# Two slots for the low halves of weights instead of three, five raw slots instead of four, and a new order of heads, ups and rope tables

## The reference

```python
def first_block(x, ...):                       # one layer
    u = rmsnorm(x, norm_mix)
    u_ssm, q, k, v = split(u @ w_in)           # 4 x 512
    y_ssm = s5_branch(u_ssm, ...)              # complex state space, 32 groups x 64 states, gelu,
                                               # y * sigmoid(y @ w_glu + b_glu)
    y_attn = stick_breaking_attention(q, k, v) # 8 heads of 64: z = q.k, w = exp(log_sigmoid(z)
                                               #   + sum of log_sigmoid(-z) over later keys)
    g_ssm, g_attn = split(sigmoid(u @ w_gate + b_gate))
    merged = g_ssm * (y_ssm @ w_up_ssm) + g_attn * (y_attn @ w_up_attn)
    h = x + merged @ w_out
    hid = relu(rmsnorm(h, norm_mlp) @ w_ff1)   # 1024 -> 4096
    h = h + (hid * hid) @ w_ff2
    return rmsnorm(h, norm_final)

def second_block(x, c, positions, ...):        # two layers
    cos, sin = rope_tables(positions)
    for l in range(2):
        shift, scale, gate = split(silu(c) @ w_ada + b_ada)
        u = x * (1 + scale) + shift
        a_in, a_gate, b_in, b_gate, q_lat, kv_lat, k_rope, c_gate, merge = split(u @ w_in)
        y_a = (silu(layer_norm(conv31(a1 * sigmoid(a2)))) * silu(a_gate)) @ w_a_out
        y_b = (gb * conv3(gc * xb) * silu(b_gate)) @ w_b_out
        y_c = (latent attention with rope, 8 heads * silu(c_gate)) @ w_c_out
        m = sum of sigmoid(merge parts) * (y_a, y_b, y_c)
        x = layer_norm(alpha * x + gate * (m @ w_o))
    return x
```

## Time and profile before

| | |
|---|---|
| median of 3 runs | 1069.53 us (1066.78 to 1070.15) |
| the profiled execution | 1071.31 us, of which the span is 1069.6 us |
| mean granted TensorE clock | 0.98 of full |
| instructions | 19601 |

### The profile page before, as it was taken

One profiled execution on the slowest core, in us unless ns is written; L12 is line 12 of the kernel. 1 busy time (PEld: TensorE's weight loads), 2 busy tenths in 40 slices (PEclk: granted clock), 3 DMA queues, 4 the chain that ended last, 5 costly groups with the idle time before them and its releaser, 6 DMA issues.

```text
span 1069.6 us, 19601 instructions
## 1 busy us (share of the span) xinstructions
PE 1020.7 (95%) x8132; PEld 960.3 (90%) x8132; DVE 696.7 (65%) x1052; ACT 545.7 (51%) x631; POOL 376.4 (35%) x159
## 2 busy tenths in 40 slices
PE   7998999889999999999999999999999999999996
PEld 6985777779899999989999999999789999999995
DVE  4958788773435322345977986856449789877563
ACT  5455554744544444446654744644366456446442
POOL 3079673003487888710056530000100456300000
PEclk8998999999999999999999999999899999999998
DMA  8642444664774656553744555554556444564601
GB/s 278 197 159 81 157 157 159 222 212 158 242 231 126 194 193 187 186 175 123 237 129 148 161 175 178 160 195 158 153 163 203 153 130 150 182 192 147 209 19 40
DMA packets 159496, 179.58 MB, mean 168 GB/s; under 512 B 5040, under 2 KB 141744, under 8 KB 159408
## 3 DMA queue, kind: packets, MB, share of 16 engines
q1 hardware_dynamic: 159024, 177.22, 52.0%
q0 software_dynamic: 384, 1.10, 0.3%
HBM read 177.26 MB, written 1.05 MB: 167 GB/s over the span
## 4 chain that ended last, share of the span: by engine, by line
PE 76%; DVE 9%; issue 7%; ACT 5%; DMA 2%; POOL 1%; SPq 0%; DVEq 0%; ACTq 0%; POOLq 0%
PE pg L1791 64%; DVE p_bu L1669 2%; ACT w_hi L924 2%; PE p_s L1874 2%; DVE area L1243 2%; PE p_y L1949 1%; ACT u_hi L899 1%; PE pg L1812 1%; PE p_s L1767 1%; DVE area L1261 1%; PE p_s L1928 1%; DVE rows L1285 1%; DVE area L1247 1%; DMA area<-in_c_state 1%; PE p_bu L1928 1%
## 5 line engine op out<-in xcount | busy, mean ns | idle before, releaser
L814 POOL TENSOR_TENSOR w_lo<-raw,w_hi 128x2048 fp32r<-128x2048 f32 x61 | 285.3, 4688 | 316.9 <-ACT w_hi L924 316.9
L924 ACT ACTIVATE w_hi<-raw 128x2048 fp32r<-128x2048 f32 (+3 forms) x153 | 275.1, 1804 | 67.5 <-PE pg L1791 29.3
L1234 DVE TENSOR_TENSOR w_lo<-raw,w_hi 128x2048 fp32r<-128x2048 f32 (+2 forms) x92 | 190.7, 2084 | 61.0 <-ACT w_hi L924 60.8
L1791 PE MATMUL pg<-u_hi,w_hi 128*128 128x256 f32 x1536 | 213.5, 291 | 16.7 <-ACT u_hi L899 11.0
L1791 PEld LDWEIGHTS pg<-u_hi,w_hi 128*128 128x128 f32 x1536 | 195.9, 193 | 27.2 <-issue 11.4
L1791 PE MATMUL pg<-u_lo,w_hi 128*128 128x256 f32 x1536 | 202.9, 285 | 0.0
L1791 PE MATMUL pg<-u_hi,w_lo 128*128 128x256 f32 x1536 | 200.2, 283 | 0.0
L1791 PEld LDWEIGHTS pg<-u_lo,w_hi 128*128 128x128 f32 x1536 | 194.3, 195 | 0.0
L1791 PEld LDWEIGHTS pg<-u_hi,w_lo 128*128 128x128 f32 x1536 | 191.4, 192 | 0.0
L930 ACT ACTIVATE area<-pg 128x512 f32<-128x512 f32 (+1 forms) x92 | 54.1, 588 | 155.5 <-PE pg L1791 143.6
L1669 DVE SCALAR_TENSOR_TENSOR p_bu<-area,par,p_bu 128x256 f32<-128x256 f32 x232 | 93.9, 483 | 0.8
(11 more groups left out here) (221 smaller groups left out, 1343.6 us busy)
## 6 DMA issues: line engine op xcount, KB each, us to landing
raw<-in_w_in SPq DMA_DIRECT2D x68, 1024.0 KB, 5.4
raw<-in_w_ff SPq DMA_DIRECT2D x32, 1024.0 KB, 5.6
raw<-in_w_ada SPq DMA_DIRECT2D x24, 1024.0 KB, 5.3
raw<-in_w_gate SPq DMA_DIRECT2D x8, 1024.0 KB, 7.8
raw<-in_w_o SPq DMA_DIRECT2D x8, 1024.0 KB, 5.2
raw<-in_w_out SPq DMA_DIRECT2D x4, 1024.0 KB, 8.7
raw<-in_w_b_out SPq DMA_DIRECT2D x4, 1024.0 KB, 5.1
raw<-in_w_c_out SPq DMA_DIRECT2D x4, 1024.0 KB, 5.5
```

The source lines that it names most:

```text
L814: pool.tensor_tensor(w_lo[:, s, 0:n], raw[:, r, 0:n], w_hi[:, s, 0:n].bitcast(F32), ALU.subtract).then_inc(sem(f"raw_free{r}"), 1)
L924: act.activation(dst, src, ACT.Copy).then_inc(*(c.event("w_hi", q["s"]) if i == len(parts) - 1 else c.step()))
L1234: ins = dve.tensor_tensor(dst, src, hi.bitcast(F32), ALU.subtract)
L1791: ins = pe.matmul(pg[g % 2][0:m, i * T:i * T + T], w[:, k, a:a + m], x[:, k, :], start=x is x_hi and w is wh and (i, k) == turns[0], stop= ...
```

## The change

`raw` gets five slots, `w_lo` two (`LO`), `w_hi` keeps three. The window of the look-ahead is a constant of its own (`AHEAD` = 4), so the halves are issued as far ahead as before. The low halves of `up_attn` 0 and 1, `up_ssm` 0 and 1, `out` 0 and 1 and `glu` 0 move from VectorE to GpSimd (68 there instead of 61). The bu matmuls no longer stand between the two z matmuls of `stick_scores`; the outputs of two heads are made together (`stick_out` for even heads only, once for two). `high_ahead` stands before `s5_y`. `rope_tables` is cut in four steps, one after each of the ff1 panels 4 to 7, and `modulate_columns` comes two chunks later. The weights, products and bytes are the same.

```diff
@@ slots and the list
-POOL_LOW = [("gate", n) for n in range(3, 8)] + [(job, n) for job in ("ff1", "ff2") for n in range(2 * DFF // W)]
+POOL_LOW = [("gate", n) for n in range(3, 8)] + [(job, n) for job in ("up_attn", "up_ssm", "out") for n in range(2)] + [("glu", 0)] + [(job, n) for job in ("ff1", "ff2") for n in range(2 * DFF // W)]
-RAW = 4
+RAW = 5
 HL = 3
+LO = 2
+AHEAD = 4
@@ the order: heads
         if m + 1 < HEADS:
             step("stick_scores", m + 1)
-        else:
-            step("bu", 2 * m + 1)
+        step("bu", 2 * m + 1)
...
+        if m and m % 2 == 0:
+            step("stick_out", m - 2)
...
-        if m:
-            step("stick_out", m - 1)
-    step("stick_out", HEADS - 1)
+    step("stick_out", HEADS - 2)
     step("ada_turn", 10)
     step("s5_out", HEADS - 1)
     step("split", "ctx")
+    step("high_ahead", count["split"] + 2)
     step("s5_y", WT - 1)
...
-    step("high_ahead", count["split"] + 2)
@@ the order: feed-forward
                 panel("ff1", 0, 2 * c + n, "w_ff1", 0, W * c + 256 * n, KT, 256, 1)
+                if c in (2, 3):
+                    step(("rope_angles", "rope_reduced", "rope_half", "rope_tables")[2 * c - 4 + n])
...
-        if c == 2:
-            step("rope_tables")
+        if c == 4:
             step("modulate_columns", 0)
@@ the waits of a low half (GpSimd, and VectorE alike)
-                    past = SPLIT[q["s"] - HL]
+                    past = SPLIT[q["s"] - LO]
                     pool.wait_ge(sem("groups"), past["g"] + past["groups"] - 1 + 1)
...
-            within = RAW if PANELS[at]["split"] else 1 if PANELS[at]["layer"] and PANELS[at]["n"] in (7, 11) else 2
+            within = AHEAD if PANELS[at]["split"] else 1 if PANELS[at]["layer"] and PANELS[at]["n"] in (7, 11) else 2
@@ TensorE, heads
             def stick_scores(hd, _):
...
-                if hd:
-
-                    bu_ready(2 * hd - 1)
-                    bu_part(2 * hd - 1, 0)
                 pe.matmul(p_z[:, 0:T], k1[rows, f, 0:P], q1[rows, f, :], start=True, stop=True)
-                if hd:
-                    bu_part(2 * hd - 1, 1).then_inc(*event("bu", 2 * hd - 1))
                 pe.matmul(p_z[:, T:T + P], k1[rows, f, P:T], q1[rows, f, P:T], start=True, stop=True).then_inc(*event("z", hd))
...
             def stick_out(hd, _):
-                pe.wait_ge(sem("w_stick"), over("w_stick", hd))
+                pe.wait_ge(sem("w_stick"), over("w_stick", hd + 1))
...
-                weighted_values(v1, stick_w[:, hd % 2], hd).then_inc(*event("o_stick", hd))
+                weighted_pair(v1, stick_w, hd).then_inc(*event("o_stick", hd // 2))
@@ VectorE, rope
-            def rope_tables(_, __):
+            def rope_angles(_, __):
...
                 ts(nmean[rows], nmean[rows], freq[rows, 0:1], None, ALU.mult).then_inc(*c.step())
+            def rope_reduced(_, __):
                 turns(nmean[rows], sin_cos[rows], cos_sin[rows])
+            def rope_half(_, __):
                 ts(nmean[rows], sin_cos[rows], 0.5, None, ALU.mult).then_inc(*c.event("rope_angle"))
+            def rope_tables(_, __):
                 dve.wait_ge(sem("rope_sines"), over("rope_sines"))
```

More of the change, by code:

```diff
@@ L640, in slot @@
         def slot(tensor, q):
-            n = q["index"] % RAW if tensor is raw else q["s"] % HL
+            n = q["index"] % RAW if tensor is raw else q["s"] % (HL if tensor is w_hi else LO)
             cols = q["cols"] if tensor is raw else twice(q["cols"]) if q["job"] in TWICE else q["cols"]
@@ L649, in halves_of @@
                 n = q["kt"] * q["cols"]
-                at = q["index"] % RAW if tensor is raw else q["s"] % HL
+                at = q["index"] % RAW if tensor is raw else q["s"] % (HL if tensor is w_hi else LO)
                 return [tensor[:, at, 0:n]]
@@ L807, in low_halves @@
                     pool.wait_ge(sem("w_hi"), over("w_hi", q["s"]))
-                    past = SPLIT[q["s"] - HL]
+                    past = SPLIT[q["s"] - LO]
                     pool.wait_ge(sem("groups"), past["g"] + past["groups"] - 1 + 1)
                     n = q["kt"] * q["cols"]
-                    r, s = q["index"] % RAW, q["s"] % HL
+                    r, s, low = q["index"] % RAW, q["s"] % HL, q["s"] % LO
                     if q["job"] == "xb":
                         pool.wait_ge(*k.last)
-                    pool.tensor_tensor(w_lo[:, s, 0:n], raw[:, r, 0:n], w_hi[:, s, 0:n].bitcast(F32),
+                    pool.tensor_tensor(w_lo[:, low, 0:n], raw[:, r, 0:n], w_hi[:, s, 0:n].bitcast(F32),
                                        ALU.subtract).then_inc(sem(f"raw_free{r}"), 1)
@@ L1210, in _ @@
                          stick_scores=stick_scores, stick_weights=stick_weights, stick_out=stick_out,
-                         rope_tables=rope_tables, prescale=prescale, latent_sums=latent_sums,
+                         rope_half=rope_half, prescale=prescale, latent_sums=latent_sums,
                          latent_roots=latent_roots, scores=scores, turn=turn, ln_a_squares=ln_a_squares, ln_a_var=ln_a_var,
@@ L1493, in stick_weights @@
                 if hd >= 2:
-                    dve.wait_ge(sem("o_stick"), over("o_stick", hd - 2))
+                    dve.wait_ge(sem("o_stick"), over("o_stick", (hd - 2) // 2))
                 tt(stick_w[:, hd % 2], p_c[:, 0:384], stick_z[hd % 2], ALU.add).then_inc(*c.event("logw", hd))
@@ L1603, in rope_tables, with rope_half @@
                 ts(nmean[rows], nmean[rows], freq[rows, 0:1], None, ALU.mult).then_inc(*c.step())
+            def rope_reduced(_, __):
+                rows = slice(NOPE, P)
                 turns(nmean[rows], sin_cos[rows], cos_sin[rows])
+            def rope_half(_, __):
+                rows = slice(NOPE, P)
                 ts(nmean[rows], sin_cos[rows], 0.5, None, ALU.mult).then_inc(*c.event("rope_angle"))
+            def rope_tables(_, __):
+                rows = slice(NOPE, P)
                 dve.wait_ge(sem("rope_sines"), over("rope_sines"))
@@ L1751, in _ @@
                          stick_scores=stick_scores, stick_soft=stick_soft, stick_weights=stick_weights,
-                         ada_end=ada_end, glu_mul=glu_mul, gate_take=gate_take, modulate=modulate, rope_tables=rope_tables, u2_piece=u2_piece, modulate_columns=modulate_columns,
+                         ada_end=ada_end, glu_mul=glu_mul, gate_take=gate_take, modulate=modulate, rope_angles=rope_angles, rope_reduced=rope_reduced, rope_half=rope_half, rope_tables=rope_tables, u2_piece=u2_piece, modulate_columns=modulate_columns,
                          latent_norm=latent_norm, rope_k=rope_k, rope_q=rope_q, conv_a=conv_a, conv_b=conv_b, scores=scores,
@@ L1915, in s5_turn, with bu @@
                 ins.then_inc(*event("bt_ps"))
-            def bu_ready(r):
+            def bu(r, _):
                 pe.wait_ge(sem("bt"), over("bt", 1))
@@ L1924, in bu_ready @@
                     pe.wait_ge(sem("root"), over("root", ("norm", 0)))
-            def bu_part(r, comp):
                 f, rows = r // FOUR, slice(32 * (r % FOUR), 32 * (r % FOUR) + 32)
-                return pe.matmul((p_bu, p_s)[r % 2][:, T * comp:T * comp + T], bt[rows, comp, f, :], ussm[rows, f, :],
-                                 start=True, stop=True)
-            def bu(r, _):
-                bu_ready(r)
-                bu_part(r, 0)
-                bu_part(r, 1).then_inc(*event("bu", r))
+                bank_ = (p_bu, p_s)[r % 2]
+                for comp in range(2):
+                    ins = pe.matmul(bank_[:, T * comp:T * comp + T], bt[rows, comp, f, :], ussm[rows, f, :],
+                                    start=True, stop=True)
+                ins.then_inc(*event("bu", r))
             def s5_out(j, _):
@@ L1988, in weighted_pair @@
                 return ins
[L1990 to L1994 removed]
             def stick_out(hd, _):
[L1997 removed]
+                pe.wait_ge(sem("w_stick"), over("w_stick", hd + 1))
                 for s, v in emptied(groups_of("v")):
                     pe.wait_ge(s, v)
[L2000 removed]
+                if hd:
                     pe.wait_ge(sem("ctx"), over("ctx", hd // 2 - 1))
[L2002 removed]
+                weighted_pair(v1, stick_w, hd).then_inc(*event("o_stick", hd // 2))
             def latent_stats(l, _):
```

19 lines of the change are left out of this document (6 added, 13 removed).

## The result

The changed kernel takes 1121.37 us (1116.46 to 1124.39, 4 runs) against 1069.05 before: 1.0488 times as long, 95% interval 1.0445 to 1.053. Slower was forecast, but +33 us, not +52; the time lies above the range, which ended at 1112. The profiled execution is the fastest of the four, 1116.46 us with a span of 1114.7, so its trace explains 45 of the 52 us. Of the other 7, 4.9 are the step from this execution to the median of the four, and 2.3 the step from the profiled execution of the kernel before down to its own median.

A forecast was written before the change was run, and what follows sets the result against it. TensorE's stream plus its waits was taken as the bound, busy 1020.7 of 1069.6 us. Terms 1.2-4.5+4+19+13 = +33 gave 1104 profiled, 1102 as median; own range 1092 to 1112, widened to 1066 to 1112.

The forecast's parts named there:

- A: Start: VectorE's low half at 42.51 must wait for the running panel's end, delaying the state-space set-up: +1.2 us.
- B: Heads: regrouped z and bu matmuls gain 0.38 per iteration and paired head outputs gain 2.1: together -4.5 us.
- C: Ups and outs: an old wait goes, but GpSimd's lows hold VectorE's products and a low delays out 1: +4 us.
- D: Feed-forward: GpSimd's lows hold v_lo and the rope steps, so takes come late: +19 us, at the least +4.
- The v_lo term: Feed-forward: v_lo of a chunk's second ff1 panel is held, TensorE resumes 0.5 late in five chunks: 2.5 us.
- rope_reduced: Feed-forward rope step of five short operations: the first waits, the rest meet another GpSimd low: +6.5 us, at least 2.8.
- rival 1: Feed-forward: rope operations slip into gaps between GpSimd's lows, so +4 there, +18 in all, 1088 us; chance 0.23.
- E: The two layers: low halves wait for running panels at ag, convolution, a1 and merge: 6.6 a layer, +13 us.
- The convolution's cause: Layers: the low at 627.04 waits 4.5 for its panel, the convolution ends about 5 later, layer-norm sums wait 2.8.
- Rival 3: Long waits bring TensorE's lower granted clock, 1.5 us more at each of five or so: 1110 us; chance 0.12.
- Rival 2: Waits fall into idle time of VectorE and GpSimd; only gains at heads and ups show: about 1063 us; chance 0.17.
- point of decision: Faster if feed-forward v_lo ends before +4.9 of its panel and no VectorE low waits over 1 us before a take.

The follow-up runs named there:

- Heads only: Kernel before with only the heads' new order, pairs and early high halves; slots, GpSimd's list and rope as before: 1059.80 us, 0.9902.
- rope only: Kernel before with only the rope steps cut in four: 1093.14 us, 1.0202.
- the slots alone: Kernel before with five raw slots, two low-half slots and the look-ahead of four, nothing else: 1114.86 us, 1.0424.

## Why the prediction was wrong

Direction, bound and both mechanisms (a low half that waits for the running panel; GpSimd's hold on VectorE) were right. The sum was 12 us short in the traced execution and 19 by the median. By its terms:

- **A** (+1.2): right; the lag grew by 1.3 from the sixth panel to the heads, and 0.6 to 0.9 stood there before any slot mattered.
- **B** (-4.5): the 0.38 per iteration was right. Heads only gave -6.5 there; in the trace before, the granted clock was 0.66 from 145 to 150 us, in heads only 1.00, which is part of the difference. The changed kernel's -11.4 has 4.7 of the scatter above: its profiled execution waited 0.76 at 96 us, not 2.25. That is luck for the forecast, not a right step, and it is in one trace alone: that this execution was the fastest of its four fits, and the other three have no trace.
- **C** (+4): 10.9, of which 1.7 behind the outs, in the norm. The gain (2.4 to 2.9) came with heads only (3.2), but not here: over up_attn, where heads only gained 3.2, the changed kernel lost 2.1. The term had one hold of 1.3 there; the traces show three, with TensorE idle 1.58, 1.39 and 2.63. The three holds of the merged products were priced at +2.4 in all, and one of them alone (232.71) made TensorE wait 3.72, then ran it at the lower clock (238.55: 3.62 us for sixteen where 2.08 is usual), which the term did not hold.
- **D** (+19): 24.8. The v_lo term was 0.5 a chunk, measured 0.5 to 0.9; rope_angles 2.9, measured 2.89; rope_half and rope_tables 9.2, measured 8.78. rope_reduced was wrong by its whole 6.5: it cost nothing, because GpSimd with two slots waits for the same stalled TensorE, as rival 1 had it for all steps. Instead came twice 2.4 us of lower clock, and 6.2 at the end of the feed-forward, overlooked.
- **E** (+13): 18.6, of which 4.9 are lower clock; the waits themselves make 13.7. ag's 1.5 is there, and behind its wait of 3.02 another 1.5 of lower clock. a1's 0.7 and the convolution's 2.8 (2.7 measured) were right. The merge was 1.6 in the second layer, as forecast; in the first the clock fell after it, and it was 3.1. The convolution's cause was not the one given: the low at 627.04 never waited, and GpSimd's hold at 667.52 made the 2.7 us.

The step that failed is where the waits were turned into a sum and a range. **Rival 3**, the lower clock after long waits, was treated as another case with a chance of 0.12, though the likeliest sum itself held waits of 2.9 and 9.2 us, beyond the 2.44 that had brought the clock down in the earlier trace rows. It was no rival but part of the forecast. Summed over the block products behind 200 us, matmuls that started 0.19 us or more after the one ahead of them, with no gap, where 0.12 is usual, cost 19.9 us in the changed kernel's trace and 8.3 before: 12 us (1 in the ups, 6 in the feed-forward, 5 in the layers), and 1.3 to 2.4 per long wait where 1.5 was assumed. C had even taken 1.5 of lower clock off. Without the clock the terms are off by +1.0 (A), -6.9 (B), +4.6 (C), -0.1 (D) and +0.7 (E). That these nearly cancel is chance: 4.7 of B is scatter, and in D what was overlooked at the feed-forward's end stands against rope_reduced. So the size of the clock's part is measured, but that it alone equals the traced miss is not a proof that nothing else was wrong.

A second step failed in C and D. The rule by which the panels with two groups should have been found stood in the prediction itself (behind a low half that waits on VectorE's queue stands the take of the running panel), and was applied to the layers and to one out panel, not to ff2 or up_attn. Issuing the take first is worth 20 us with the slots alone and 13 in the changed kernel.

Rival 2 (faster) was wrong, and its point of decision right: v_lo ended at +5.5, not before +4.9.

## What to carry to other kernels

A buffer ring one slot shorter makes its producer wait for the consumer's *current* step; count what stands behind that wait in the producer's queue, above all a drain of something that finished half a step earlier, and issue the drain first. The fastest version here is the kernel before with only the heads' new order and early high halves, 1059.80 us (0.9902). Before short operations are spread over a stretch to fill gaps, see what another engine's long instruction does to each of them: in one burst one of the rope operations was held a little (the cast, 0.63 us for 0.29); as four steps, two were held in the changed kernel and four in rope only, for 4.5 to 4.7 us each. And a long wait of TensorE can be paid twice, once as the wait and once as 1.3 to 2.4 us of lower clock behind it: such a term belongs into the sum, not among the rivals.
